# The bias line sent between two row halves, a seventh expert block in a free area, and a gather with its high parts first

## The chip, the core and the metric

The kernel runs on one core of a Trainium2 chip. The metric is the device time of one execution in microseconds. Five engines work side by side: TensorE (PE, with its weight loads PEld), VectorE (DVE), ScalarE (ACT), GpSimd (POOL) and SyncE (SP). They meet through semaphores. Transfers run on 16 DMA engines. SyncE's transfers form the queue q1, ScalarE's the queue q10.

## What is computed

The reference is a stack of two models on 256 tokens of width 1024, in fp32. Cut to what matters here:

```
# first block
z   = rms_norm(x) @ w_in                    # 1024 -> 1440: q_a, k_a, v_a, c_q, c_kv, k_rope
o_a = window attention(q_a, k_a, v_a)       # + rel_bias[t5_bucket(j - i)] on every score
o_b = latent attention(c_q, c_kv, k_rope)
x   = x + concat(norm(o_a), norm(o_b)) @ w_o
h2  = rms_norm(x)
aff = softmax(h2 @ w_router)                # 16 experts
gate, idx = top_k(aff.T, 32)                # every expert chooses 32 tokens
xe  = h2[idx]
ye  = (silu(xe @ w_gate) * (xe @ w_up)) @ w_down * gate
x   = x + scatter_add(ye)
# second block, two layers: mod = silu(c) @ ada_w + ada_b, four times; S5 mixer, conv FFN,
# forgetting attention, conv FFN, final norm
```

Each of the 16 experts has three weights of 1024 x 1024: 12 MB, six blocks of 2048 KB.

## The kernel before

Every engine has one hand-written program, and the order of work is the order of its lines. Weights come through `ring`, six slots of 16 KB per partition. `weight_plan` (L143) writes down the order of all loads and the slot of each. SyncE's program goes through this order in one loop: `begin` waits until what was last in the slot has been used (`released`, L210, says by which semaphore), and then the load is issued (L576). All loads are in this one queue, so a load that waits holds back all behind it.

Stages, in order:

- **First projection.** `x` is turned, and z is made in three column blocks (512, 512, 416), each in two row halves of 128 tokens (t = 0, 1). Block 0 is a plain fp32 product; blocks 1 and 2 work with high and low fp32r parts. ScalarE makes the high part of a weight block (`win_high`), VectorE the low one (`win_low`). The high part of block 2 goes to slot 0, so the load of block 2 waits for `z_mm` 2, both row halves of block 0.
- **The bias table.** One small product on TensorE (`line_mm`) makes a line of 511 values for each of 8 heads, and ScalarE copies it out, writes it to `bias_line` in DRAM and waits until it is there. Then it reads it back as `Lb`, 128 partitions x 8 heads x 384 values, each partition shifted by one (the spread, semaphore `line_spread`). The first `scores` wait for it.
- **Attention** in steps s = 0 to 7 of four heads (0 to 3 window attention, 4 to 7 latent attention). A step turns probabilities, spreads the inverse sums, makes the next step's scores, some filler product (`latent_product`, `wo_group`) and then its `outputs`.
- **ada.** 24 blocks of `ada_w` are multiplied with silu(c), six for each layer (`ada_product(n)`), then `ada_turn(layer)`. Products 0 to 11 are spread over the first block as fillers, each 16 matmuls on a ring block.
- **Routing.** The residual is turned and normed, logits, softmax, a search for the top 32 on VectorE, and from it the one-hot matrix `GallR`. The gather multiplies the rows, split in `xgh` and `xgl`, with `GallR`: eight chunks c of 128 features, each two row halves times two parts, into bank c % 7 of PSUM, and ScalarE copies each chunk out.
- **Experts.** For each expert six grouped products, j = 0 and 1 gate, 2 and 3 up, 4 and 5 down. Product j reads the ring slot of block j and frees it with `expert_mm`. In between are the sums, silu, and the scatter. GpSimd makes tables for the S5 stage beside them, one for every second expert. SyncE loads the next expert's block j when the current one's block j has been used.
- Then the S5 mixer, FFN, attention and FFN of the second block.

The order of the loads of interest in `weight_plan` before:

```
load("ada", 1, to=1); load("ada", 1, to=3)      # 4, 5
load("ada", 1, to=2); load("ada", 1, to=3); load("ada", 1, to=0)   # 6, 7, 8
load("ada", 1, to=1); load("ada", 1, to=2)      # 9, 10
load("expert", 2, NE, to=4)
load("ada", 1, to=3)                            # 11
load("expert", 4, NE, to=0)
```

Here are the functions that the change touches.

Of the kernel before, what the change touches and what calls it, by code (L numbers as in the profile page):

```python
# [20 lines left out]
F32 = mybir.dt.float32  # L21
# [8 lines left out]
P = 128  # L30
# [30 lines left out]
NE = 16  # L61
# [81 lines left out]
def weight_plan():  # L143
# [5 lines left out]
    def load(name, n=1, times=1, apart=False, to=None):  # L149
# [3 lines left out]
        first = sum(k[0] == name for k in order)  # L153
# [12 lines left out]
    def high_in(name, i, slot):  # L166

        high_slot[name, i] = slot
        before[name, i].append(holds[slot])
        holds[slot] = (name, i)  # L170
# [15 lines left out]
    load("ada", 1, to=3)  # L186
    load("ada", 1, to=0)
    load("ada", 1, to=1)
    load("ada", 1, to=2)
    load("expert", 2, NE, to=4)  # L190
    load("ada", 1, to=3)
    load("expert", 4, NE, to=0)
# [49 lines left out]
def build(nc, x, cons, cols, rows, relb, wrt, wff, bf16z, w_in, w_qb, w_kvb, w_o, w_gate, w_up, w_down, ada_w,  # L242
# [4 lines left out]
    with ExitStack() as ctx:  # L247
# [211 lines left out]
        xgh = SPLIT[:, 2 * D:2 * D + NT * D]  # L459
# [102 lines left out]
        def _(sp):  # L562
# [38 lines left out]
            for name, i in order:  # L601
# [4 lines left out]
                elif name == "ada":  # L606
                    load(begin(name, i), SLOT, block(ada_w, i))
                elif name == "qkvb":
# [3 lines left out]
                elif name == "expert":  # L612
                    begin(name, i)
                    expert(0, i)
                    if i == SLOTS - 1:
                        with sp.Fori(1, NE) as e:
                            for j in range(SLOTS):

                                sp.wait_ge(S("expert_mm"), e * SLOTS + (j + 1 - SLOTS))
                                expert(e, j)  # L620
                elif name == "s5":
# [19 lines left out]
        def _(pe):  # L641
# [123 lines left out]
            pe.wait_ge(S("line_loaded"), 32)  # L765
            mm(ps[0:AH, 6, 0:LINE], rb[:, :], K("onehot", BUCKETS + 1), True, True).then_inc(S("line_mm"), 1)
# [216 lines left out]
            for s in range(4, 8):  # L983
# [12 lines left out]
                if s == 5:  # L996
                    ada_turn(0)
                pe.wait_ge(S("r_copied"), s + 1)
                outputs(2 * s)
                outputs(2 * s + 1)  # L1000
            ada_product(6)
# [8 lines left out]
            ada_product(7)  # L1010
# [5 lines left out]
            ada_product(8)  # L1016
# [4 lines left out]
            for n in (9, 10, 11):  # L1021
                ada_product(n)
# [7 lines left out]

            pe.wait_ge(S("routed"), 4)
            pe.wait_ge(S("rows_low"), 1)
            for c in range(NC):
                if c == 7:

                    pe.wait_ge(S("xe_copied"), 1)
                for t in range(NT):
                    for part in (xgh, xgl):
                        last = mm(ps[:, c % 7, :], part[:, t * D + c * P:t * D + c * P + P], GallR[:, t, :],
                                  t == 0 and part is xgh, t == 1 and part is xgl)  # L1040
                last.then_inc(S("xe_mm"), 1)
# [4 lines left out]
            def expert(i, b):  # L1046
# [4 lines left out]
                def grouped(j, lhs, bank, first):  # L1051

                    w = filled("expert", j, i * 2 + b).rearrange("p (c n) -> p c n", c=4)
# [53 lines left out]
            with pe.Fori(0, NE // 2) as i:  # L1107
                for b in range(2):
                    expert(i, b)
# [177 lines left out]
        def _(act):  # L1287
# [135 lines left out]

# [67 lines left out]
            for s in range(4, 8):  # L1491
# [3 lines left out]
                if s > 4:  # L1495
                    spread_copied(s - 1)
# [1188 lines left out]
```

## Time and profile before

| | |
|---|---|
| median of three runs | 1448.74 us (1446.78 to 1451.35) |
| the profiled execution | 1453.92 us, its span 1452.1 us |
| TensorE busy | 1238.7 us, 85% |
| VectorE / ScalarE / GpSimd busy | 659.9 / 464.0 / 269.7 us |
| mean granted clock of TensorE | 0.888 of full speed |
| DMA | 369.62 MB, 255 GB/s in the mean |

A busy share is a mean over stages with different limits. The span is the profiled program on the core; the time of the execution has a little more around it. Times in the rows count from the start of the span.

### The profile page before, as it was taken

The numbers are of one execution on the slowest core, as the hardware profiler recorded it, in microseconds if no ns is written. First come the engines' busy times: TensorE is split into PE (matmuls) and PEld (weight loads), VectorE is DVE, ScalarE is ACT, GpSimd is POOL, SyncE is SP. The second block draws the span as 40 slices with busy tenths as digits, with TensorE's granted clock in tenths as the row PEclk, the third lists the DMA queues.
The fourth block names the chain that finished last, engine by engine and source line by source line (L and its number), as shares of the span: only waits on it lengthen the run. The fifth ranks groups of instructions, "written<-read, shape, count | busy, mean of one in ns | idle before, by whom it ended". The sixth has DMA issues, their size and how long they took to land.

```text
span 1452.1 us, 21871 instructions
## 1 busy us (share of the span) xinstructions
PE 1238.7 (85%) x8746; PEld 875.1 (60%) x8746; DVE 659.9 (45%) x1158; ACT 464.0 (32%) x682; POOL 269.7 (19%) x289
## 2 busy tenths in 40 slices
PE   7699988878788886887886779999969989899997
PEld 4455444333333332426655768999959767799995
DVE  2476452211211121214345636777763255676676
ACT  4364421111111111105313415444343243544442
POOL 0000376321303303113113600000016420000000
PEclk9899988987988898877976988999989959899998
DMA  6845699999999999993962214454344301355541
GB/s 247 370 174 232 246 397 429 428 428 429 427 429 429 428 429 429 428 429 148 395 247 107 88 58 160 178 200 182 147 174 153 138 30 35 132 196 194 196 173 44
DMA packets 36000, 369.62 MB, mean 255 GB/s; under 512 B 4069, under 2 KB 5614, under 8 KB 12270
## 3 DMA queue, kind: packets, MB, share of 16 engines
q1 hardware_dynamic: 33552, 364.66, 61.9%
q10 hardware_dynamic: 2398, 4.27, 0.8%
q8 instruction: 35, 0.57, 0.2%
q14 instruction: 15, 0.12, 0.0%
HBM read 367.84 MB, written 1.06 MB: 254 GB/s over the span
## 4 chain that ended last, share of the span: by engine, by line
PE 54%; DMA 28%; DVE 7%; ACT 4%; POOL 3%; issue 3%; DVEq 0%; SPq 0%; ACTq 0%; POOLq 0%
PE ps L649 52%; DMA ring<-in_w_up 24%; DMA W<-bias_line 2%; DMA ring<-in_w_in 1%; PE ps L664 1%; ACT ring_parts L488 1%; DVE W L2447 1%; PE ps L875 1%; DMA ring<-in_s_out 1%; DMA ring<-in_fox_in 1%; POOL ring_parts L496 0%; ACT XH L1352 0%; DVE ss L1913 0%; DVE W L2468 0%; DMA bias_line<-W 0%
## 5 line engine op out<-in xcount | busy, mean ns | idle before, releaser
L649 PE MATMUL ps<-W_parts 128*128 128x256 f32 (+1 forms) x2672 | 390.8, 309 | 8.7 <-issue 4.4
L649 PEld LDWEIGHTS ps<-W_parts 128*128 128x128 f32 x2672 | 363.2, 194 | 35.4 <-issue 10.3
L649 PE MATMUL ps<-ring,W 128*32 128x512 f32 (+2 forms) x1640 | 269.2, 721 | 77.5 <-DMA ring<-in_w_up 47.4
L649 PEld LDWEIGHTS ps<-ring,W 128*32 128x32 f32 (+1 forms) x1640 | 70.3, 131 | 249.9 <-issue 152.3
L649 PE MATMUL ps<-W 128*32 128x64 f32 (+7 forms) x1696 | 151.3, 324 | 51.6 <-DVE W L2455 22.5
L496 POOL TENSOR_TENSOR ring_parts<-ring,ring_parts 128x2048 fp32r<-128x2048 f32 x18 | 98.3, 5471 | 367.1 <-ACT ring_parts L488 330.3
L649 PEld LDWEIGHTS ps<-W 128*32 128x32 f32 (+5 forms) x1696 | 97.8, 178 | 110.4 <-issue 94.3
L2481 DVE TENSOR_TENSOR W_parts<-ring,W_parts 128x2048 fp32r<-128x2048 f32 x44 | 100.9, 2292 | 29.7 <-ACT W_parts L1645 29.7
L649 PE MATMUL ps<-XH_parts,ring_parts 128*128 128x256 f32 x512 | 96.6, 292 | 7.8 <-issue 5.0
L2362 DVE COPY W<-ps 128x1024 f32<-128x1024 f32 x16 | 19.6, 1224 | 173.7 <-PE ps L649 173.7
L649 PEld LDWEIGHTS ps<-kc,W 128*128 128x128 f32 x648 | 82.9, 209 | 10.4 <-issue 6.6
L649 PEld LDWEIGHTS ps<-XH_parts,ring_parts 128*128 128x128 f32 x512 | 83.4, 200 | 8.7 <-issue 5.6
L649 PE MATMUL ps<-kc,W 128*128 128x32 f32 (+2 forms) x648 | 84.1, 290 | 2.9 <-POOL W L1840 2.9
L1645 ACT ACTIVATE W_parts<-ring 128x2048 fp32r<-128x2048 f32 x44 | 83.6, 1900 | 0.0
L649 PE MATMUL ps<-ring_parts,W_parts 128*128 128x512 f32 (+1 forms) x256 | 72.3, 404 | 10.2 <-DVE W_parts L2470 10.2
L649 PE MATMUL ps<-W_parts,ring_parts 128*128 128x256 f32 x256 | 74.5, 291 | 0.0
L649 PEld LDWEIGHTS ps<-ring_parts,W_parts 128*128 128x128 f32 x256 | 49.7, 195 | 21.9 <-DVE W_parts L2470 10.4
L1847 POOL COPY W<-XH 128x256 f32<-128x256 f32 x14 | 5.6, 400 | 284.3 <-PE ps L649 284.3
L488 ACT ACTIVATE ring_parts<-ring 128x4096 fp32r<-128x4096 f32 x14 | 50.6, 3613 | 15.9 <-DMA ring<-in_fox_in 8.8
L2366 DVE COPY W<-ps 128x512 f32<-128x512 f32 x16 | 11.1, 692 | 95.4 <-PE ps L649 95.4
L2379 DVE TENSOR_TENSOR X<-X,ps 128x512 f32<-128x512 f32 x64 | 44.0, 687 | 22.9 <-PE ps L649 22.9
L2487 DVE TENSOR_TENSOR W_parts<-ring,W_parts 128x1024 fp32r<-128x1024 f32 x44 | 53.6, 1218 | 0.7 <-ACT W_parts L1653 0.7
(370 smaller groups left out, 1359.0 us busy)
## 6 DMA issues: line engine op xcount, KB each, us to landing
ring<-in_w_gate SPq DMA_DIRECT2D x32, 2048.0 KB, 22.2
ring<-in_w_up SPq DMA_DIRECT2D x32, 2048.0 KB, 26.5
ring<-in_w_down SPq DMA_DIRECT2D x32, 2048.0 KB, 23.4
ring<-in_ada_w SPq DMA_DIRECT2D x24, 2048.0 KB, 11.0
ring<-in_up SPq DMA_DIRECT2D x44, 1024.0 KB, 5.4
ring<-in_dn SPq DMA_DIRECT2D x44, 512.0 KB, 3.3
ring<-in_fox_in SPq DMA_DIRECT2D x6, 2048.0 KB, 8.2
ring<-in_w_in SPq DMA_DIRECT2D x2, 2048.0 KB, 13.7
```

The lines of the kernel that those rows point to most:

```text
L488: act.activation(ringr[:, high_slot[name], :], ring[:, slot_of[name], :], ACT.Copy).then_inc(S("w_high"), 1)
L496: eng.tensor_tensor(ringr[:, slot_of[name], a], ring[:, slot_of[name], a], ringr[:, high_slot[name], a].bitcast(F32), ALU.subtract).then_i ...
L649: return pe.matmul(o, l, r, start=a, stop=z_, skip_group_check=True, **kw)
L664: last = pe.transpose(ps[:, banks[c // 2], (c % 2) * T + t * P:(c % 2) * T + t * P + P], src[:, t, c * P:c * P + P], ident)
L875: last = pe.transpose(ps[:, 4 + g % 2, o:o + P], Pex[:, 2 * (g % 4) + h, kb * P:kb * P + P], ident)
L1645: act.activation(uh[:, b], ring[:, slot_of[name, b], 0:2048].rearrange("p (a n) -> p a n", a=2), ACT.Copy).then_inc(S("up_high"), 1)
L2362: v.tensor_copy(Us.rearrange("p (b n) -> p b n", b=2), ps[:, 2:4, :]).then_inc(S("u_copied"), 1)
L2366: v.tensor_copy(Ys[:, BANK:D], ps[:, 6, :]).then_inc(S("y1_copied"), 1)
L2379: tt(xs_part, xs_part, ps[:, k, :], ALU.add).then_inc(S("x_added"), 1)
L2447: last = tt(to[:, s], g, turn, ALU.mult)
L2481: tt(ul[:, b, :, :], ring[:, slot_of[f"up{k}", b], 0:2 * D].rearrange("p (a n) -> p a n", a=2), uh[:, b, :, :].bitcast(F32), ALU.subtract) ...
L2487: tt(dl[:, b, :], ring[:, slot_of[f"down{k}", b], 0:D], dh[:, b, :].bitcast(F32), ALU.subtract).then_inc(S("down_low"), 1)
```

## The change

1. `line_mm` is made after the row half t = 0 of projection block 0 instead of after t = 1. ScalarE copies the line out and sends it to DRAM before it copies the two halves of block 0 out. It asks for the spread behind these two copies (n == 0), not behind those of block 1, and makes `win_high(2, ...)` after that.
2. Block 0 of expert 0's `w_gate` is loaded into `O_`, the first 4096 columns of W, which is free from the last query turn (`qkb_turned` 4) until the S5 tables. Its request stands behind that of `ada` block 8. Slot 0 so begins with expert 1's block 0; the other five blocks of expert 0 and `ada` blocks 6 to 11 have other slots. The first two experts stand outside TensorE's loop. `ada_turn(0)` moves from step 5 to step 4, `ada_product(6)` and `(7)` into steps 6 and 7, in front of the outputs, and the later products move up by one.
3. The high parts of seven chunks are gathered first, then their low parts, then chunk 7. `xgh` lies in XH with the chunks apart. ScalarE makes it after the exponentials instead of before them, and VectorE makes `xgl` after `GallR` instead of before the search.

```diff
@@ weight_plan
     load("ada", 1, to=2)
-    load("ada", 1, to=3)
     load("ada", 1, to=0)
     load("ada", 1, to=1)
+    load("ada", 1, to=3)
     load("ada", 1, to=2)
-    load("expert", 2, NE, to=4)
-    load("ada", 1, to=3)
-    load("expert", 4, NE, to=0)
+    load("ada", 1, to=0)
+    for i, slot in ((1, 4), (2, 5), (3, 1), (4, 3), (5, 2)):
+        load("expert", 1, NE, to=slot, first=i)
+    load("expert", 1, NE - 1, to=0, first=0)
@@ SyncE
                     load(begin(name, i), SLOT, block(ada_w, i))
+                    if i == 8:
+
+                        sp.wait_ge(S("qkb_turned"), 4)
+                        sp.dma_start(O_, block(w_gate, 0)).then_inc(S("first_loaded"), 16)
...
-                    expert(0, i)
-                    if i == SLOTS - 1:
-                        with sp.Fori(1, NE) as e:
-                            for j in range(SLOTS):
-
+                    expert(0 if i else 1, i)
+                    if i == 0:
+
+                        with sp.Fori(1, NE - 1) as e:
+                            for j in range(1, SLOTS):
                                 sp.wait_ge(S("expert_mm"), e * SLOTS + (j + 1 - SLOTS))
                                 expert(e, j)
+                            sp.wait_ge(S("expert_mm"), e * SLOTS + 1)
+                            expert(e + 1, 0)
+                        for j in range(1, SLOTS):
+                            sp.wait_ge(S("expert_mm"), (NE - 2) * SLOTS + j + 1)
+                            expert(NE - 1, j)
@@ TensorE, first projection
-            pe.wait_ge(S("line_loaded"), 32)
-            mm(ps[0:AH, 6, 0:LINE], rb[:, :], K("onehot", BUCKETS + 1), True, True).then_inc(S("line_mm"), 1)
+                if t == 0:
+                    pe.wait_ge(S("line_loaded"), 32)
+                    mm(ps[0:AH, 6, 0:LINE], rb[:, :], K("onehot", BUCKETS + 1), True, True
+                       ).then_inc(S("line_mm"), 1)
@@ TensorE, steps 4 to 7
-                if s == 5:
+                if s == 4:
                     ada_turn(0)
+                elif s > 5:
+                    ada_product(s)
                 pe.wait_ge(S("r_copied"), s + 1)
                 outputs(2 * s)
                 outputs(2 * s + 1)
-            ada_product(6)
             wo_group(6)
@@ TensorE, gather
             pe.wait_ge(S("routed"), 4)
+            pe.wait_ge(S("rows_high"), 1)
+            for c in range(7):
+                gather(c, "high", True, False)
             pe.wait_ge(S("rows_low"), 1)
...
+            for c in range(7):
+                gather(c, "low", False, True).then_inc(S("xe_mm"), 1)
+            pe.wait_ge(S("xe_copied"), 1)
+            gather(7, "high", True, False)
+            gather(7, "low", False, True).then_inc(S("xe_mm"), 1)
@@ ScalarE, first projection
+            act.wait_ge(S("line_mm"), 1)
+            act.activation(lineS[:, 0:LINE], ps[0:AH, 6, 0:LINE], ACT.Copy).then_inc(S("line_copied"), 1)
+            act.wait_ge(S("line_copied"), 1)
+            act.dma_start(line_dram[:, 0:LINE], lineS[:, 0:LINE]).then_inc(S("line_written"), 16)
             act.wait_ge(S("rs_ready"), 1)
...
                 if n == 0:
-                    win_high(2, 0)
-                    win_high(2, 1)
-                if n == 0:
-                    act.wait_ge(S("line_mm"), 1)
-                    act.activation(lineS[:, 0:LINE], ps[0:AH, 6, 0:LINE], ACT.Copy).then_inc(S("line_copied"), 1)
-                    act.wait_ge(S("line_copied"), 1)
-                    act.dma_start(line_dram[:, 0:LINE], lineS[:, 0:LINE]).then_inc(S("line_written"), 16)
-                if n == 1:
                     act.wait_ge(S("line_written"), 16)
                     act.dma_start(Lb[:, :, :], bass.AP(line_dram.tensor, 0, [[1, P], [BANK, AH], [1, 384]])
                                   ).then_inc(S("line_spread"), 16)
+                    act.wait_ge(S("z_mm"), 2)
+                    win_high(2, 0)
+                    win_high(2, 1)
@@ ScalarE, routing
-            act.activation(xgh, XNf, ACT.Copy).then_inc(S("rows_high"), 1)
             act.wait_ge(S("routed"), 1)
...
+            for t in range(NT):
+                last = act.activation(xgh[:, :, t, :], XN[:, t, :].rearrange("p (c m) -> p c m", c=NC), ACT.Copy)
+            last.then_inc(S("rows_high"), 1)
             ada_copy(1)
@@ VectorE, routing
-            v.wait_ge(S("rows_high"), 1)
-            tt(xgl, XNf, xgh.bitcast(F32), ALU.subtract).then_inc(S("rows_low"), 1)
             v.wait_ge(S("route_mm"), 2)
...
             last.then_inc(S("routed"), 1)
+            v.wait_ge(S("rows_high"), 1)
+            for t in range(NT):
+                last = tt(xgl[:, t * D:t * D + D].rearrange("p (c m) -> p c m", c=NC),
+                          XN[:, t, :].rearrange("p (c m) -> p c m", c=NC), xgh[:, :, t, :].bitcast(F32), ALU.subtract)
+            last.then_inc(S("rows_low"), 1)
```

## Rows read from the trace of the kernel before

**Rows 1.** windows: start:end, us, busy time by engine, clock, DMA share, GB/s

```profile
...
18.50:30.00 11.50, 11.50 (x28) 4.65 (x27) 4.63 (x4) 6.24 (x6) 0.00 (x0) 1.00 0.08 15
30.00:51.00 21.00, 21.00 (x108) 17.89 (x110) 10.58 (x16) 7.54 (x9) 0.00 (x0) 1.00 0.97 401
...
54.00:68.00 14.00, 0.45 (x2) 0.48 (x4) 1.75 (x7) 2.35 (x4) 0.00 (x0) 0.64 1.02 431
...
142.00:159.00 17.00, 15.86 (x83) 7.41 (x81) 8.61 (x26) 5.98 (x17) 0.00 (x0) 1.00 0.00 0
...
250.00:600.00 350.00, 282.31 (x1871) 121.41 (x1863) 71.03 (x124) 49.50 (x68) 77.02 (x102) 0.85 1.01 428
```

**Rows 2.** chain that ended last, 600 to 700 us: start us, us, what

```profile
...
611.48 27.33 DMA ring<-in_w_up
```

**Rows 3.** timeline of PE, 0 to 80 us: start us, us, engine, operation, idle before

```profile
...
28.64 1.02 PE L649 MATMUL ps<-kc,rb 33*8 33x511 f32 x2
...
67.55 2.08 PE L649 MATMUL ps<-W 64*128 64x256 f32 x8 [14.33 <-DMA W<-bias_line]
69.56 2.30 PE L801 MATMUL ps<-kc,W 128*128 128x128 f32 x10
```

**Rows 4.** timeline of ACT, 0 to 100 us

```profile
...
44.08 0.41 ACTq L1421 DMA_DIRECT2D W<-bias_line  x1
...
54.40 0.47 ACT L1454 ACTIVATE W<-ps,pc 128x256 f32<-128x256 f32 x1
```

**Rows 5.** DMA issues, 28 to 70 us: size, us from issue to landing

```profile
...
W<-bias_line ACTq DMA_DIRECT2D x1, 1536.0 KB, 23.3
```

**Rows 6.** DMA queues, 51 to 54 and 54 to 58 us: packets, MB, share

```profile
...
q10 hardware_dynamic: 641, 0.98, 90.5%
q1 hardware_dynamic: 19, 0.26, 21.9%
...
q1 hardware_dynamic: 95, 1.56, 91.7%
q10 hardware_dynamic: 88, 0.12, 8.0%
```

**Rows 7.** timeline of SP's queue, 0 to 260 us

```profile
...
1.67 27.39 SPq L576 DMA_DIRECT2D ring<-in_w_in  x3
...
50.15 0.81 SPq L576 DMA_DIRECT2D ring<-in_ada_w  x2
...
203.22 2.05 SPq L576 DMA_DIRECT2D ring<-in_w_gate  x2
```

**Rows 8.** timelines of PE and DVE, 25 to 56 us

```profile
...
40.89 0.54 PE L649 MATMUL ps<-ring_parts,XH_parts 128*128 128x416 f32 x2
...
36.96 3.69 DVE L1969 TENSOR_TENSOR ring_parts<-ring,ring_parts 128x1664 fp32r<-128x1664 f32 x2 [12.19 <-ACT ring_parts L1384]
```

**Rows 9.** timeline of PE, 160 to 262 us

```profile
...
173.99 3.61 PE L649 MATMUL ps<-ring,silz 128*32 128x512 f32 x16
...
189.85 9.74 PE L649 MATMUL ps<-W_parts 128*128 128x512 f32 x32 [2.38 <-DVE W_parts L2306]
201.08 7.07 PE L649 MATMUL ps<-ring,W 128*32 128x512 f32 x64 [1.50 <-POOL W L1780]
```

**Rows 10.** timeline of PE, 140 to 162 us

```profile
...
145.89 1.09 PE L649 MATMUL ps<-W 128*64 128x128 f32 x16 [0.32 <-ACT W L1364]
...
156.25 1.92 PE L649 MATMUL ps<-ring,silz 128*32 128x512 f32 x16
159.04 3.24 PE L649 MATMUL ps<-ring,W 128*128 128x512 f32 x7 [0.87 <-ACT W L1376]
```

**Rows 11.** timelines of DVE and ACT in the routing and gather

```profile
...
178.66 2.28 DVE L2290 TENSOR_TENSOR W_parts<-XH,W_parts 128x2048 fp32r<-128x2048 f32 x1
...
174.30 1.91 ACT L1521 ACTIVATE W_parts<-XH 128x2048 fp32r<-128x2048 f32 x1
...
199.62 0.69 ACT L1533 ACTIVATE XH<-ps,pc 128x512 f32<-128x512 f32 x1 [0.22 <-PE ps L649]
```

**Rows 12.** timeline of PE in the second expert

```profile
...
246.10 3.68 PE L649 MATMUL ps<-kc,W 128*128 128x64 f32 x16 [2.90 <-POOL W L1840]
```

More of the change, by code:

```diff
@@ L147, in weight_plan, with load @@
     uses, holds, at = [0] * SLOTS, [None] * SLOTS, 0
-    def load(name, n=1, times=1, apart=False, to=None):
+    def load(name, n=1, times=1, apart=False, to=None, first=None):
         nonlocal at
         at = at if to is None else to
-        first = sum(k[0] == name for k in order)
+        first = sum(k[0] == name for k in order) if first is None else first
         for i in range(first, first + n):
@@ L168, in high_in @@
         high_slot[name, i] = slot
-        before[name, i].append(holds[slot])
         holds[slot] = (name, i)
@@ L455, in build @@
         xl = low_at(OT_AT)
-        xgh = SPLIT[:, 2 * D:2 * D + NT * D]
+        xgh = XHr[:, NT * D:2 * NT * D].rearrange("p (c t m) -> p c t m", c=NC, t=NT)
         xgl = SPLIT[:, 4 * D:4 * D + NT * D]
@@ L1009, in _ @@
             turn(0, X, (4, 5, 6, 2), "x_added")
-            ada_product(7)
+            ada_product(8)
             ht_ready(0)
@@ L1015, in _ @@
             last.then_inc(S("route_mm"), 1)
-            ada_product(8)
+            ada_product(9)
             pe.wait_ge(S("routed"), 2)
@@ L1020, in _ @@
             last.then_inc(S("route_mm"), 1)
-            for n in (9, 10, 11):
+            for n in (10, 11):
                 ada_product(n)
@@ L1028, in _, with gather @@
             last.then_inc(S("route_mm"), 1)
+            def gather(c, part, first, last_):
+                for t in range(NT):
+                    rows_ = xgh[:, c, t, :] if part == "high" else xgl[:, t * D + c * P:t * D + c * P + P]
+                    last = mm(ps[:, c % 7, :], rows_, GallR[:, t, :], first and t == 0, last_ and t == 1)
+                return last
             pe.wait_ge(S("routed"), 4)
+            pe.wait_ge(S("rows_high"), 1)
+            for c in range(7):
+                gather(c, "high", True, False)
             pe.wait_ge(S("rows_low"), 1)
[L1033 to L1041, printed above, removed]
+            for c in range(7):
[3 more added lines that the diff above has]
+            gather(7, "low", False, True).then_inc(S("xe_mm"), 1)
             pe.wait_ge(S("xe_copied"), 8)
@@ L1051, in grouped @@
                 def grouped(j, lhs, bank, first):
-                    w = filled("expert", j, i * 2 + b).rearrange("p (c n) -> p c n", c=4)
+                    if j:
+                        w = filled("expert", j, i * 2 + b)
+                    elif isinstance(i, int) and i * 2 + b == 0:
+                        pe.wait_ge(S("first_loaded"), 16)
+                        w = O_
+                    else:
+                        w = filled("expert", 0, i * 2 + (b - 1))
+                    w = w.rearrange("p (c n) -> p c n", c=4)
                     for n in range(2):
@@ L1105, in expert @@
                     pe.wait_ge(S("kc_copied"), i + 1)
-            with pe.Fori(0, NE // 2) as i:
+            for b in range(2):
+                expert(0, b)
+            with pe.Fori(1, NE // 2) as i:
                 for b in range(2):
@@ L1496, in _ @@
                     spread_copied(s - 1)
+                if s == 5:
+                    ada_keep(0)
                 if s == 6:
-                    ada_keep(0)
                     act.wait_ge(S("o_copied"), 6)
@@ L2309, in _ @@
             last.then_inc(S("routed"), 1)
+            v.wait_ge(S("rows_high"), 1)
+            for t in range(NT):
+                last = tt(xgl[:, t * D:t * D + D].rearrange("p (c m) -> p c m", c=NC),
+                          XN[:, t, :].rearrange("p (c m) -> p c m", c=NC), xgh[:, :, t, :].bitcast(F32), ALU.subtract)
+            last.then_inc(S("rows_low"), 1)
             def modulation(kept, a, b):
```

## The prediction

> **What bounds the kernel now.** I read the page's slices first, then `windows` over the stages, then the waits, and only then single instructions. The span falls into three kinds of stretch. In the sixteen experts the DMA engines are full: between 250 and 600 us they move 428 GB/s at a share of 1.01, while TensorE is busy for 282 of 350 us [rows 1]. The chain of work says the same: the last wait for a third projection block lasts 27.33 us and is a DMA [rows 2]. A 2048 KB block at 428 GB/s takes 4.9 us, so what is worth something there is a block that need not be moved in that stretch, or an earlier start of it. After the experts, and in the attention before them, TensorE sets the pace and everything behind it moves as one. The one large hole outside the experts is TensorE's wait for the bias table: 14.33 us, until 67.55 [rows 3].
>
> Why is that table late? ScalarE asks for the table, one row of 384 values per head spread to all partitions, at 44.08 [rows 4], and it takes 23.3 us to land [rows 5]. It is only 1536 KB, 3.7 us of a full DMA. It waits because it shares the engines. It consists of 128 x 8 pieces of 1,536 bytes, 64 for each of 16 engines; a block of SyncE's queue consists of 128 rows of 16 KB, 8 for each engine. Look at the packets by queue. From 51 to 54 us ScalarE's queue (q10) gets 641 packets and SyncE's (q1) only 19: there SyncE's queue was empty. From 54 to 58, with both filled, it is 88 against 95, one for one, and a pair costs an engine 4 x 16 / 95 = 0.67 us [rows 6]. So most of the table went through in a hole of 3 us, and the rest crept.
>
> **Part 1, the line sent between the row halves.** The line's product moves in front of the second row half. That half then ends 1.0 us later (the 1.02 us of the product at 28.64) [rows 3], and so do the two things that wait for it: SyncE's third projection load, whose issue ends at 29.06 now [rows 7], and ScalarE's copy of the second half. The write to DRAM goes out near 24, into an idle DMA (0.08 of its share from 18.5 to 30) [rows 1], and is back long before 30. But the table is asked for only behind ScalarE's copy of the second half: near 30.4, instead of 44.08. That is 0.7 us behind SyncE's load of 29.7, and two blocks of `ada` are in the same burst. From there SyncE's queue holds the third projection block, two `ada` blocks, `w_qb` and `w_kvb`, 8 packets each: 40 per engine.
>
> Now the sum of the queue. Before, this stream ran from about 30 to 51 and then left the hole until the next blocks, issued at 50.15 [rows 7], arrived at 54. After, it starts 1.0 us later and carries 35 to 39 packets of the table between its own, at 0.07 us each (3 us x 16 / 641) [rows 6]: 2.5 us. It ends at 54 to 54.5, and the next blocks are there: the hole is closed. 25 to 29 table packets per engine are left, and the queue holds 24 more of SyncE's (two `ada`, one `w_o`). At 0.67 us a pair that is 16 us and more: the table lands between 69 and 71.5, where all else that was issued lands. The lower end is an engine that still sees half a microsecond of hole, the upper one the slowest engine; the slowest decides, so I take 70.5. A second view of the same: the engines are full from 30 to 68 before and after [rows 1], carry the same bytes, and start 1.0 us later. So TensorE starts the scores 3.0 us **later** than at 67.55. The later landing of the third projection block (by 1.5 us) is hidden: VectorE ends its low half at 40.65, which becomes about 42.2, and TensorE, which begins this block at 40.89 with 0.54 us for each pair of products, reaches the half at about 43 [rows 8]. If this cover were short, the loss would be its excess.
>
> The Trainium skill (DMA: Bandwidth & Descriptors, Queues, rings and completion order) says that an engine takes turns between the queues, but drains a whole packet of some 9 to 17 descriptors before it switches. By it eight turns or fewer would serve the table, and the line would not be late at all (that is the first rival). The counts of the trace, 95 to 88, speak for one descriptor a turn.
>
> **Part 2, the seventh block.** `w_gate` block 0 goes to a free area as soon as the query turns are done, into DMA time that is partly idle (nothing moves from 142 to 159) [rows 1]. It leaves 87 blocks instead of 88 between the refill and the last awaited one: -4.9 us. But the first expert's first product now frees no slot; SyncE waits for the second. The refill began at 203.22, 2.1 us behind TensorE's start at 201.08 [rows 7, 9]; four products take 7.07 us [rows 9], so it is now 3.9 us behind: +1.8. The price is also TensorE's: `ada` products 6 and 7 stand in front of the outputs of steps 6 and 7. One costs 1.92 us; step 6 has 0.32 us of wait to hide it, step 7 none. Product 6 stood in front of the wait for `o_scaled`, which still ended last by 0.87 us [rows 10]: taking it out of there shortens nothing. I add 1.6 + 1.8 = +3.4. Bounds: 0 (hidden) to 3.8. `ada_turn` moved by one step lies in VectorE's waits: 0.
>
> **Part 3, the gather.** VectorE's subtraction (2.28 us) leaves the routing chain, and ScalarE's high copy (1.91 us) goes behind the exponentials [rows 11]. TensorE's `ada` product of 3.61 us ends at 177.6 [rows 9] and stands in front of the transposes, so it, not the sum of both, limits: VectorE's search starts near 178.1 instead of 180.94. -2.8 us. The low parts must then be made beside 14 high products; these take 14/32 of 9.74 us, 4.3 us [rows 9], the subtraction about 2.4: covered. But ScalarE's eight copies now start only behind the high parts: 8 x 0.69 = 5.5 us behind 4.5 make 10.0, where the gather took 9.74 and one copy (10.4) [rows 9, 11]. With hand-over times I take +0.5, between 0 and 1. So the experts start at 201.08 + 3.4 - 2.8 + 0.5 = 202.2.
>
> Refill: 202.2 + 3.9 = 206.1 against 203.22, +2.9; minus 4.9 gives **-2.0 us** for parts 2 and 3, between -5 (products hidden, copies not bunched) and 0. The cover is not wide: in expert 1 TensorE waits 2.90 us for GpSimd's table [rows 12], and the third expert's first slot comes free about 1 us before the DMA would run dry.
>
> **Sum.** +3.0 - 2.0 = +1.0 us on the profiled span of 1452.1. The profiled execution took 1453.92 against a median of 1448.74, so I put the sum on the median: **1449.7**, own range 1446.5 to 1452.5. The three runs shown are 4.6 us apart; 0.3% (4.3 us) is about what can be told from no change.
>
> **Rivals.**
> (a) *The table lands early* (0.25). If an engine serves several table packets a turn, or SyncE's second `ada` request waits behind the table's 1024 pieces so that a hole opens at 41, the table is there before 55. Then TensorE starts behind ScalarE's key copy, which ends at 54.87 [rows 4]: 12.7 us earlier. The granted clock, 0.64 in the mean of the wait [rows 1], need not fall to 1.2 GHz then: the first scores take 2.08 us and the turns behind them 2.30 [rows 3], at 2.4 GHz about half, so some 2 us more. -14.7 - 2.0: **1432**. For it: 3.7 us of bytes. Against it: the one-for-one counts.
> (b) *Half a hole* (0.13): a hole of 1 to 2 us stays at 54, even on the slowest engine; 15 to 29 packets slip through and the table lands at 58 to 66. -2 to -9 and -2: about **1441**.
> (c) *Slower* (0.10): the experts' refill is tied to TensorE, not to the count of blocks. If the path in front of the experts grows by more than 1 us beyond my sum, the slot for expert 3's first block comes free after the queue has run dry, and the -4.9 is given back; with the table at 71.5 this is +4 + 1.5: **1454**.
> (d) The forecast itself: 0.52.
>
> Faster by over 0.3% (below 1444.4): (a) and most of (b), 0.35. Within: (d) and the rest, 0.54. Slower: 0.11. For eight in ten the range must take in (a) and reach (c): 1431 to 1454.
>
> **What the profile after would show.** Right: the line's DMA near 24, the table's request near 30.4, but a landing time of about 40 us instead of 23.3, TensorE's wait 17 us, half clock until the scores. Between 51 and 54 q1 is not empty. SyncE's first refill 3.9 us behind the first expert product, a DMA gap of about 10 us before it. `ada` products inside steps 6 and 7 with no shorter wait for `o_scaled`. The routed search some 2.8 us nearer to the residual sum. Wrong: scores before 60, or a landing time under 25 us: then the sharing between the queues was misread, and this one term decides the sign of all.

## The result, and the profile after

The changed kernel takes 1436.4 us (median of six runs, 1428.91 to 1438.76), the kernel before 1450.49 us (six runs, 1446.78 to 1452.26). The ratio is 0.9897 [0.9875, 0.9919]: about 14 us or 1.0% **faster**, and the interval does not reach 1. I had forecast 1449.7 us and no difference that can be told. The profiled execution took 1438.76 us, its span is 1437.0 us, 15.1 us shorter than the 1452.1 us of before.

First the windows of the changed kernel, with the columns of [rows 1]:

```profile
18.50:30.00 11.50, 11.50 (x27) 4.42 (x26) 4.59 (x3) 6.21 (x6) 0.00 (x0) 1.00 1.00 412
30.00:42.00 12.00, 12.00 (x51) 9.35 (x50) 6.68 (x8) 4.34 (x4) 0.00 (x0) 1.00 0.58 211
...
142.00:159.00 17.00, 14.28 (x58) 6.21 (x57) 3.32 (x8) 3.74 (x9) 0.00 (x0) 0.90 0.48 165
```

The first line is the surprise. Between 18.5 and 30 us the DMA had a share of 0.08 before [rows 1]; now it is 1.00. Nothing that I had costed moves bytes there. SyncE's queue says what it is (start, us, operation):

```profile
1.67 1.85 SPq L576 DMA_DIRECT2D ring<-in_w_in  x3
3.56 1.01 SPq L576 DMA_DIRECT2D ring<-in_ada_w  x2
42.21 0.33 SPq L576 DMA_DIRECT2D ring<-in_w_qb  x1
```

The three projection loads were issued over 27.39 us [rows 7], because the third waited for the two row halves of block 0. Now all three are out at 3.52, and the two `ada` blocks behind them at 4.57. They are in before 33 us. In the third line `ada` and expert blocks move where nothing moved before, asked for near 147 and at 156.17; the seventh block itself is asked for already at 100.53, not in that gap. Next ScalarE's timeline, then the transfers from 33 to 41 us, and TensorE's timeline:

```profile
24.57 0.30 ACTq L1432 DMA_DIRECT2D bias_line<-W  x1
24.98 0.69 ACT L1441 ACTIVATE W<-ps,rs 128x512 f32<-128x512 f32 x1 [0.43 <-ACT W L1430]
31.02 0.69 ACT L1441 ACTIVATE W<-ps,rs 128x512 f32<-128x512 f32 x1 [5.36 <-PE ps L658]
33.30 0.41 ACTq L1445 DMA_DIRECT2D W<-bias_line  x1
33.81 3.08 ACT L1412 ACTIVATE ring_parts<-ring 128x1664 fp32r<-128x1664 f32 x2 [2.10 <-DMA bias_line<-W]
```

```profile
q10 hardware_dynamic: 1040, 1.57, 57.8%
...
W<-bias_line ACTq DMA_DIRECT2D x1, 1536.0 KB, 7.6
```

```profile
56.23 1.92 PE L658 MATMUL ps<-W 64*128 64x256 f32 x8 [1.90 <-ACT W L1481]
58.08 2.15 PE L812 MATMUL ps<-kc,W 128*128 128x128 f32 x10
```

The table is asked for at 33.30 and lands 7.6 us later, at 40.9. In those 8 us SyncE's queue, q1, has no packet at all; beside q10 there is only one packet of instructions. Before it took 23.3 us [rows 5]. So TensorE no longer waits 14.33 us for the bias table [rows 3] but 1.90 us for ScalarE's key copy, and starts the scores at 56.23 instead of 67.55: 11.3 us earlier.

Behind that the two kernels run nearly in step. TensorE, the refill, and the chain's last wait for a third projection block:

```profile
171.09 3.64 PE L658 MATMUL ps<-ring,silz 128*32 128x512 f32 x32
...
184.42 3.35 PE L658 MATMUL ps<-W_parts 128*128 128x512 f32 x14
...
190.71 1.92 PE L658 MATMUL ps<-W 128*32 128x512 f32 x16 [2.01 <-ACT XH L1563]
```

```profile
174.78 20.14 SPq L576 DMA_DIRECT2D ring<-in_w_gate  x2
196.25 1.91 SPq L576 DMA_DIRECT2D ring<-in_w_up  x2
```

```profile
599.52 25.76 DMA ring<-in_w_up
...
644.76 3.61 ACT ring_parts L488
```

The experts start at 190.71, 10.4 us earlier than in [rows 9], of which 11.3 came from the scores: 0.9 us were lost between. The first refill is the second of the two `w_gate` requests, issued about 194.6 (3.9 us behind the experts' start) against 203.22 [rows 7]: 8.6 us earlier. The last awaited block lands at 599.52 + 25.76 = 625.3 against 638.8 [rows 2]: 13.5 us, which is 8.6 and one block of 4.9. The last 1.6 us of the 15.1 come from behind it.

### The profile page after: what moved, and what is told of

Its sections match the earlier page's. It is cut to its first block, busy times and chain, and to the rows that moved or that the text cites. A ratio compares the mean times of both kernels' runs of the same rounds, so it can differ in the third digit from the quotient of the medians.

```text
span 1437.0 us, 21864 instructions
## 1 busy us (share of the span) xinstructions
PE 1232.7 (86%) x8746; PEld 876.6 (61%) x8746; DVE 668.7 (47%) x1159; ACT 463.6 (32%) x683; POOL 270.9 (19%) x289
## 4 chain that ended last, share of the span: by engine, by line
PE 58%; DMA 24%; DVE 7%; ACT 4%; POOL 3%; issue 3%; DVEq 0%; SPq 0%; ACTq 0%; POOLq 0%
PE ps L658 56%; DMA ring<-in_w_up 22%; ACT ring_parts L488 1%; PE ps L673 1%; DMA ring<-in_w_in 1%; DVE W L2480 1%; PE ps L886 1%; DMA ring<-in_fox_in 1%; DMA ring<-in_s_out 1%; POOL ring_parts L496 0%; DVE ss L1943 0%; DVE W L2501 0%; DVE XH L2078 0%; ACT XH L1380 0%; PE ps L898 0%
## 5 line engine op out<-in xcount | busy, mean ns | idle before, releaser
L658 PE MATMUL ps<-W_parts 128*128 128x256 f32 (+1 forms) x2656 | 385.4, 308 | 7.3 <-DVE W_parts L1970 3.1
L658 PEld LDWEIGHTS ps<-W_parts 128*128 128x128 f32 x2656 | 359.0, 193 | 32.2 <-issue 10.8
L658 PE MATMUL ps<-ring,W 128*32 128x512 f32 (+2 forms) x1624 | 265.7, 714 | 71.7 <-DMA ring<-in_w_up 39.3
L658 PE MATMUL ps<-W 32*128 32x64 f32 (+8 forms) x1712 | 149.2, 313 | 43.0 <-DVE W L2488 24.4
L658 PEld LDWEIGHTS ps<-W 32*128 32x128 f32 (+5 forms) x1712 | 94.4, 165 | 101.5 <-issue 85.1
L658 PEld LDWEIGHTS ps<-kc,W 128*128 128x128 f32 x648 | 88.4, 221 | 13.3 <-issue 13.3
L658 PE MATMUL ps<-kc,W 128*128 128x32 f32 (+2 forms) x648 | 89.3, 300 | 5.3 <-POOL W L1870 5.3
L1699 ACT ACTIVATE XH<-ps 128x256 f32<-128x256 f32 x44 | 16.9, 384 | 117.2 <-PE ps L658 117.2
```

Source lines behind the costliest of these rows:

```text
L658: return pe.matmul(o, l, r, start=a, stop=z_, skip_group_check=True, **kw)
L1699: act.activation(apd[:, b, 2:2 + T], ps[:, b, 0:T], ACT.Copy).then_inc(S("a_copied"), 1)
```

## What the diff shown ahead left out

The diff ahead of the prediction is an abridged one, and one line of the change is not in it. It is this, in `weight_plan`:

```diff
     def high_in(name, i, slot):
         high_slot[name, i] = slot
-        before[name, i].append(holds[slot])
         holds[slot] = (name, i)
```

`before[name, i]` lists what SyncE waits for ahead of a load. For the third projection block the removed line had put `z_mm` 2 there, because the *high part* of the block goes to slot 0, where block 0 lies. The load itself goes to slot 2, which is free. The changed kernel instead lets ScalarE wait for `z_mm` 2 ahead of `win_high(2, ...)`, which is the instruction that writes slot 0. I had listed that wait on ScalarE and had not asked which wait it replaced. My prediction kept "SyncE's third projection load, whose issue ends at 29.06 now" as a fixed part of the front.

## Experiments

Two theories. **L (the load):** the removed wait alone makes the table early, and my sum for the rest holds. **E (the early line):** it is early because the line is sent earlier, and I misread how two queues share an engine. Where the last microseconds matter I compare places in the trace rather than times; the reason follows below.

**1. The wait put back.** The changed kernel with the removed line restored; everything else as changed.

```diff
         high_slot[name, i] = slot
+        before[name, i].append(holds[slot])
         holds[slot] = (name, i)
```

> The changed kernel with one line put back: the third projection load waits again for both row halves of block 0, as the forecast had assumed. Theory L (the freed load decides; the sharing of the DMA engines was read rightly): the table is asked for near 31, shares with 40 packets of SyncE's per engine one for one and lands between 69 and 72, so the scores start at about 71 instead of 56.2, and the time is that of the kernel before within 4 us (parts 2 and 3 give 2, the table costs 3). Theory E (sending the line early is what gains, an engine serves several table packets a turn or a hole opens): the table lands before 50, the scores start near 56, and the time is that of the changed kernel, 13 us under before.

1449.5 us (10 runs), ratio to the kernel before 1.0006 [0.9985, 1.0026]. ScalarE, the transfers of 20 to 75 us, and TensorE in this run:

```profile
24.33 0.30 ACTq L1433 DMA_DIRECT2D bias_line<-W  x1
...
30.78 0.44 ACTq L1446 DMA_DIRECT2D W<-bias_line  x1
```

```profile
W<-bias_line ACTq DMA_DIRECT2D x1, 1536.0 KB, 39.2
```

```profile
70.08 2.08 PE L659 MATMUL ps<-W 64*128 64x256 f32 x8 [16.00 <-DMA W<-bias_line]
```

This is the kernel that my prediction described. It had, with the measured values in brackets, the line's write near 24 (24.33), the request near 30.4 (30.78), a landing time of about 40 us (39.2), a wait of 17 us (16.00), the table at 70.5 (70.0) and the total at 1449.7 (1449.5). The sending of the line alone makes the scores 2.5 us later than in [rows 3], not earlier. How far one execution can be trusted here: the first kernel of experiment 5 has the front of the kernel before and starts its scores at 65.88 instead of 67.55, and against it the cost is 4.2 us. Theory E falls. The two queues at one place of it, 41 to 51 and 51 to 54 us:

```profile
q1 hardware_dynamic: 311, 3.62, 86.0%
q10 hardware_dynamic: 312, 0.48, 12.8%
```

```profile
q1 hardware_dynamic: 140, 1.05, 83.8%
q10 hardware_dynamic: 139, 0.21, 19.4%
```

311 against 312 and 140 against 139: the queues get equal numbers of packets, a row of 8 to 16 KB against 1.5 KB. Equal numbers alone would also fit turns of several packets each. The bytes of 44 to 47 us, in 40 slices of 0.075 us, tell more:

```profile
GB/s 41 457 259 478 560 1550 0 478 0 41 457 259 478 560 1550 41 437 0 41 457 259 478 560 1550 20 457 0 41 437 239 300 778 1550 20 457 0 41 437 20 519
```

The pattern comes back every nine slices, 0.68 us, which is what a pair of one 16 KB row and one piece of the table was forecast to cost (0.67), and from 44.0 to 44.7 us there are 16 packets of each queue on the 16 engines. So a turn here is one packet. The Trainium skill (DMA: Bandwidth & Descriptors, Queues, rings and completion order) gives an engine's turn as a packet of some 9 to 17 descriptors; for these two queues the measurement says otherwise, and the bytes go 7.5 to 1 (3.62 against 0.48 MB) and 5 to 1 (1.05 against 0.21 MB) against the table. From 54 to 58 us this run has 106 packets of q1 and 231 of q10. That is the rest of the old hole, not another kind of turn: from 54 to 55 us it is 30 against 151, SyncE's queue running low, and from 55 to 58 us again 76 against 80.

**2. The load freed alone.** The kernel before with only that line removed: neither the line's new place, nor the seventh block, nor the gather.

```diff
-        before[name, i].append(holds[slot])
```

> The kernel before with only the third projection load freed; the line is sent and the table asked for where they were. Theory L: the two ada blocks move in the idle DMA before 33, so that the table, asked for near 42, meets only w_qb and w_kvb (16 packets per engine) and then an empty queue until 53: it lands near 53 and the scores start near 56, 11 us earlier; time 11 to 13 us under before. Theory E: without the early line the table lands at 60 or later; at most 6 us under before.

1433.88 us, ratio 0.9919 [0.9892, 0.9945]. This one line explains most of the result (0.9897). Its table is asked for late and lands late, and it doesn't matter:

```profile
40.91 0.44 ACTq L1420 DMA_DIRECT2D W<-bias_line  x1
```

```profile
W<-bias_line ACTq DMA_DIRECT2D x1, 1536.0 KB, 11.6
```

```profile
54.93 1.14 PE L648 MATMUL ps<-W 64*128 64x256 f32 x8 [1.91 <-ACT W L1453]
```

It is there at 52.5, before ScalarE's key copy ends.

**3. Part 1 whole.** Experiment 2 with the line made and sent between the row halves and spread at n == 0.

```diff
-            pe.wait_ge(S("line_loaded"), 32)
...
+                if t == 0:
+                    pe.wait_ge(S("line_loaded"), 32)
...
+                    act.wait_ge(S("z_mm"), 2)
+                    win_high(2, 0)
+                    win_high(2, 1)
```

> The kernel before with the whole of part 1 (line between the row halves, table asked for behind block 0, load freed) and nothing of parts 2 and 3. Scores near 56.2 as in the changed kernel: 11.3 us earlier, and up to 2 more if the clock does not fall; time 11 to 13 us under before. If parts 2 and 3 gave more than the 2 us forecast, this kernel stays more than 3 us over the changed one.

1437.18 us, ratio 0.9905 [0.987, 0.9941]. The table is asked for at 33.28, 7.6 us earlier than in experiment 2, takes 7.7 us, and the scores start at 54.80 instead of 54.93. With the load freed, the line's place is worth nothing; with the load held (experiment 1) it costs 2.5 to 4.2 us.

**4. Another cause for the same hole.** Experiment 1, with SyncE's wait kept and in addition the two `ada` requests and what follows held until the table is there.

```diff
+        before[name, i].append(holds[slot])
...
+                    if i == 0:
+                        sp.wait_ge(S("line_spread"), 16)
```

> As the first kernel of this set (load waits again), but SyncE asks for ada blocks 0 and 1 only when the table has landed. Theory L: the table then shares with 8 packets per engine of the projection block alone and lands near 39, so the scores wait for ScalarE's key copy again and start near 56: the time of the changed kernel within 3 us. Rival S (the table is slow by itself, its 1,536-byte pieces or the order of its rows, whatever is beside it): it takes over 20 us again.

1435.68 us, ratio 0.9914 [0.9888, 0.9941]. The table, asked for at 29.60, lands in 11.9 us beside the third projection load alone. Now the scores wait for something else:

```profile
57.16 2.08 PE L661 MATMUL ps<-W 64*128 64x256 f32 x8 [4.24 <-DMA ring<-in_w_qb]
```

Against experiment 1 they start 12.9 us earlier. So it is the SyncE bytes in the table's path that decide, not the instant of the request.

**5. Without part 1, and without part 2.** The changed kernel with the line, the spread and SyncE's wait as before (the first), and the kernel before with parts 1 and 3 but no block in the spare area (the second).

```diff
# first
+        before[name, i].append(holds[slot])
...
# second
-                    if i == 8:
...
-                        sp.dma_start(O_, block(w_gate, 0)).then_inc(S("first_loaded"), 16)
...
```

> The changed kernel without part 1: the bias line's write and spread, the wait of the third projection load on z_mm 2, and the place of the table's ask are as in the kernel before; the seventh block in the spare area and the gather's new order stay. The forecast's sum for parts 2 and 3 alone: the experts start about 1.1 us later, the first refill 2.9 us later, one block less of 4.9 us, so -2.0 us against the kernel before (between -5 and 0). If instead the gain of the changed kernel came from parts 2 and 3, it is over 5 us under the kernel before.

> The kernel before with part 1 (the freed third projection load included) and part 3 (gather order and the search's copies), without the seventh block. If part 2 nets to nearly nothing (one block of 4.9 us less against a refill 3.9 us instead of 2.1 us behind the experts' start and the ada products between the head turns), it equals the changed kernel within 2 us. If part 2 gains by itself, it is slower than the changed kernel by over 3 us.

Without part 1: 1447.27 us, ratio 0.9998 [0.9974, 1.0022]; I had -2.0 us, and -3.8 to +3.2 us are left by the interval. The parts 2 and 3 did not make the gain. Its trace shows no gain from them either: the last awaited block lands 571.8 us behind the start of the scores, against 571.3 us in the profiled run before. Without part 2: 1434.02 us, ratio 0.9886 [0.9852, 0.9919], level with the changed kernel. In this one TensorE met a wait for an `ada` block that the changed kernel's order of loads doesn't have, and VectorE, done with the search, then waited 3.02 us for TensorE, against 0.38 us in the changed kernel run again. These 2.6 us stand against the two products that part 2 puts in front of the outputs (3.4 us in the forecast), and the experts start 131.7 us behind the scores here and 132.1 there:

```profile
167.22 1.92 PE L648 MATMUL ps<-ring,silz 128*32 128x512 f32 x16 [1.92 <-DMA ring<-in_ada_w]
```

**6. The gather as it was.** The changed kernel, with ScalarE's high copy before the exponentials, the subtraction before the search, and high and low products in turn.

```diff
             v.wait_ge(S("rows_high"), 1)
             for t in range(NT):
                 last = tt(xgl[...], XN[...], xgh[...], ALU.subtract)     # ahead of the search again
```

> The changed kernel with the gather as it was: ScalarE's high copy ahead of the exponentials, VectorE's subtraction ahead of the search, high and low product in turn. The forecast's working says 2.8 us for the subtraction and the copy in the chain and 0.5 us given back for the bunched copies: about 2.3 us slower than the changed kernel. If the subtraction only moves to another place of the chain, no difference.

1434.33 us, 0.9886 [0.9856, 0.9915], beside the changed kernel on the same chip with 1433.81 us, 0.9883 [0.9854, 0.9912] (experiment 7). The experts start at 190.51, 135.7 us behind the scores, against 132.1 there: part 3 is worth 3.6 us at this place, where I had 2.3 (some of it may be the clock: between 165 and 175 us it was 0.56 here and 0.84 there). The search starts 3.5 us nearer to the residual's turns, where 2.8 was forecast, and from the search to the experts it is 20.2 us there and 20.3 here, so the bunched copies cost nothing where I had 0.5. At the last up block 2.3 us of it are left (569.5 against 567.2 us behind the scores), and the time shows nothing of it.

**7. The changed kernel again**, as a measure for 6 and 9.

> The changed kernel once more, beside the two below on one chip, as their measure: ratio to the kernel before 0.985 to 0.992.

Ratio 0.9883, beside the 0.9897 of the first comparison.

**8. Product 7 later.** In the changed kernel `ada_product(7)` stands in front of the outputs of step 7, and TensorE then waits 2.72 us for `o_scaled`. Here it stands in that wait.

```diff
+            ada_product(7)
             wo_group(6)
```

> The changed kernel with ada product 7 moved from between the output groups to just ahead of output-projection group 6, where TensorE waited 2.72 us for o_scaled; the product itself takes 1.92 us. If TensorE's work up to there sets the search and through it the experts' start, the time is 2 to 3.6 us under that of the changed kernel. If a transfer sets the experts' start, no difference.

> The changed kernel with ada product 7 ahead of output-projection group 6 once more, with more rounds. Its first run stood at 0.9843 of the kernel before, the changed kernel at 0.9897 and 0.9883. In the trace the experts start 129.3 us behind the scores instead of 132.1, so 2.8 us (0.2%) are explained by the moved product: 0.9843 to 0.987. If more than that was gained the first time, it was scatter of the stage behind the experts, and the ratio lies at 0.986 to 0.989.

The first time 1427.76 us, 0.9843 [0.9822, 0.9863]; again 1428.5 us, 0.9883 [0.9848, 0.9918]. The wait shrinks in both traces as expected; here the changed kernel (experiment 7) and this one (second time):

```profile
148.09 3.67 PE L658 MATMUL ps<-ring,W 128*128 128x512 f32 x8 [2.72 <-ACT W L1404]
...
155.48 2.10 PE L673 MATMUL ps<-kc,X 128*128 128x128 f32 x16
```

```profile
146.01 3.67 PE L658 MATMUL ps<-ring,W 128*128 128x512 f32 x8 [0.87 <-ACT W L1405]
...
153.40 2.10 PE L673 MATMUL ps<-kc,X 128*128 128x128 f32 x16
```

TensorE is 2.1 us further at the residual's turns, 1.8 us if both are counted from the start of the scores (55.20 and 54.95). But the experts start 129.3 us behind the scores in the first trace and 132.1 us in the second, exactly as in the changed kernel. The windows of 151 to 165, 165 to 175 and 175 to 188 us, of the first and of the second trace, say why:

```profile
151.00:165.00 14.00, 12.57 (x96) 7.38 (x98) 6.71 (x18) 11.28 (x21) 9.03 (x33) 1.00 1.00 405
165.00:175.00 10.00, 6.39 (x47) 3.41 (x40) 9.17 (x22) 1.23 (x3) 8.54 (x20) 0.89 1.01 427
175.00:188.00 13.00, 11.10 (x69) 6.97 (x71) 12.32 (x23) 6.25 (x10) 9.74 (x15) 0.95 0.73 309
```

```profile
151.00:165.00 14.00, 14.00 (x86) 7.70 (x85) 6.48 (x16) 10.68 (x20) 8.95 (x32) 0.83 1.01 403
165.00:175.00 10.00, 6.68 (x49) 2.63 (x46) 8.45 (x22) 1.97 (x4) 8.38 (x22) 0.84 1.00 424
175.00:188.00 13.00, 11.04 (x40) 8.00 (x43) 12.25 (x26) 6.01 (x9) 7.08 (x13) 0.76 0.76 320
```

The granted clock is 1.00, 0.89, 0.95 in the one and 0.83, 0.84, 0.76 in the other. The 16 matmuls of the `ada` product behind the logits take 1.92 us in the first trace and 3.64 us in the second. The 1.8 us won are in the program and can be lost to the clock of one execution.

**9. The spare area for expert 0's last block**, so that the first ring slot comes free with the first product, alone and with experiment 8's move.

```diff
-    for i, slot in ((1, 4), (2, 5), (3, 1), (4, 3), (5, 2)):
+    for i, slot in ((0, 4), (1, 5), (2, 1), (3, 3), (4, 2)):
...
-                        sp.dma_start(O_, block(w_gate, 0)).then_inc(S("first_loaded"), 16)
+                        sp.dma_start(O_, block(w_down, 1)).then_inc(S("first_loaded"), 16)
...
+            pool.wait_ge(S("expert_mm"), 6)
             table(0)
```

The area holds its block longer now, so GpSimd has to wait for the last product of expert 0 before its first table. That wait is new, and in these two versions it comes with the move.

> The changed kernel with the spare area holding expert 0's last block, and so the first freed slot read two blocks earlier: the first refill is issued about 2.1 us behind the experts' start instead of 3.9 us. If the chain of refills sets the end, 1.8 us under the changed kernel. If something else does, no difference.

> The changed kernel with ada product 7 just ahead of output-projection group 6 and with the spare area holding expert 0's last block. The two steps lie one behind the other on the same path (start of the experts, then the first freed slot), so if the chain of refills sets the end their gains add: 2 to 3.6 us and 1.8 us, 4 to 5 us under the changed kernel. If one covers the other, or if the refill then meets a slot that is not yet free or a late table of GpSimd, it is no more than 3.6 us.

Alone 1429.3 us, 0.9849 [0.9825, 0.9874]; both 1432.49 us, 0.9876 [0.985, 0.9902], level with the changed kernel's 0.9883 on that chip, where 4 to 5 us less were expected. In the run with both, the refill is where it should be, 2.0 us behind the first product:

```profile
184.55 7.07 PE L655 MATMUL ps<-ring,W 128*32 128x512 f32 x64 [2.09 <-ACT XH L1561]
```

```profile
186.53 2.04 SPq L576 DMA_DIRECT2D ring<-in_w_gate  x2
```

From the experts' start to the last landed up block it takes 434.6 us (593.46 + 25.66 - 184.55) against 435.1 (596.22 + 26.20 - 187.31) in the changed kernel: of 1.8 us expected 0.5 arrive. Most of the other 1.3 us went into a hole. In the run with both, the DMA engines ran dry from 242 to 244 us, about 1.7 us of them idle:

```profile
242.00:244.00 2.00, 2.00 (x26) 0.56 (x19) 0.00 (x0) 0.00 (x0) 0.00 (x0) 1.00 0.17 66
```

SyncE asks for expert 3's first block only at 243.09, because TensorE, in expert 1, had waited 4.96 us for GpSimd's table, and the slot comes free behind that. In the changed kernel run again the wait is 3.84 us and the share from 246 to 252 us is 0.88, some 0.7 us idle, so 1.0 of the 1.3 us are in the difference. With the block's move alone the wait is 2.50 us, there is no hole (a share of 1.02 from 242 to 244), and the stretch takes 433.6 us, 1.5 less than 435.1: there the 1.8 us nearly arrive. This is the thin cover that the prediction named, "about 1 us before the DMA would run dry". In sum the last block of the run with both lands 3.1 us earlier behind the scores, and the time shows 1.3 us of it, within its scatter. None of these versions is shown to beat the changed kernel.

**Why the times scatter so.** From ScalarE's first high copy of the S5 stage to the end of the span, all of these kernels do the same work. The stretch takes 795.7 us in the profiled run before, 792.2 in the changed kernel, 789.0 in it again, and 784.9 in experiment 1, the shortest of all. In the experiments it lies between 784.9 and 792.3. That is more than the effects of parts 2 and 3. Two lines of 760 to 811 us, before and in experiment 1:

```profile
760.00:811.00 51.00, 33.98 (x508) 29.26 (x509) 29.92 (x34) 21.60 (x19) 24.72 (x9) 0.70 0.24 95
```

```profile
760.00:811.00 51.00, 32.63 (x489) 29.36 (x482) 37.98 (x33) 20.19 (x18) 29.15 (x7) 0.80 0.15 57
```

The granted clock differs, 0.70 against 0.80. That the clock alone makes the whole spread is likely and not shown.

## Why the prediction was wrong

**The step that failed** is the first of part 1: that SyncE's third projection load keeps its wait, "whose issue ends at 29.06 now", and that "That half then ends 1.0 us later ..., and so do the two things that wait for it". In the changed kernel only ScalarE's copy waits; the load is out at 3.52. Everything that followed from a queue full from 30 us on was computed for another program. In place of +3.0 us the term is -11.3 us (67.55 to 56.23) in the pair of profiled runs, and -12.6 (to 54.93) in experiment 2, which is that edit alone.

**The working on top of it was right.** Experiment 1 is that program. Measured, with the forecast in brackets: the table at 70.0 (70.5), its landing time 39.2 (40), the scores 2.5 to 4.2 us later (3.0), the total 1449.5 (1449.7). One packet in turn for each queue is confirmed by the equal counts and the period of 0.68 us. The hole was closed but for one microsecond (54 to 55). The write "back long before 30" held there; in the changed kernel it met the freed loads in its engines, and small constants in its own queue that they had held up (726 packets of q10 were through by 24 us, 910 before), and took from 24.57 to about 33.2, 8.6 us for 16 KB, which moved the request by 2.3 us and cost nothing.

**Parts 2 and 3.** In the profiled pair: experts +0.9 us relative to the scores (forecast +1.1), refill +2.7 (forecast +2.9), one block less -4.9, together -2.2 (forecast -2.0). The agreement is luck in good part. The same sum is +0.6 us for the first kernel of experiment 5 against the kernel before (571.8 against 571.3 us from the scores to the last awaited block), and -1.6 us for the changed kernel run again against experiment 3 (567.2 against 568.8). Experiment 8 shows such a sum moving by 2.8 us with the clock of one run. Over the runs the stretch from the experts' start to the last up block is 437.7, 436.7, 437.0 and 438.6 us with the old order of loads (before, 2, 3, second of 5), and 433.8 to 436.7 in the eight runs with the new one (the changed kernel twice, 1, 4, first of 5, 6, both of 8), 435.3 in the mean: -2.2 us, where 1.8 - 4.9 = -3.1 was forecast. A part of the 0.9 us that are missing is DMA idle time in front of expert 3's first block (0.7 us in the changed kernel run again, 0.5 in the first of experiment 8); the rest stays open. Part 3 came out 1.3 us larger than its term (experiment 6): 0.7 in the search, 0.5 in the copies. The `ada` products ahead of the outputs of steps 6 and 7 were sized rightly, 1.5 and 1.8 us against 1.6 and 1.8; not in the sum was that TensorE, after its wait of 2.72 us, made eight matmuls of `wo_group` 6 in 5.37 us in the profiled changed kernel, and in 3.67 us in it again.

**The rivals.** Rival (a) had the time, 1432, and its ending: the table before 55, and then ScalarE's key copy, 11.3 us earlier instead of 12.7. Of its two causes neither is the real one, but the second, "a hole opens at 41", was close in kind: the hole is at 34 to 42. I gave it 0.25. The measured 1436.4 is outside the forecast's own range, 1446.5 to 1452.5, and inside the wide one, 1431 to 1454, only because that was drawn to take in this rival. The hole of rival (c), the experts' refill tied to TensorE, is there in small: 0.7 us in the changed kernel run again, 1.7 us in the last kernel of experiment 9. The mark that I named for this case, a landing time under 25 us, is what came (7.6); the cause that I tied to it, "then the sharing between the queues was misread", did not.

**The granted clock** in the stretch 18.5 to 51 is 1.00 before and after; between 54 and 68 before it was 0.64, with TensorE busy for 0.45 of 14 us [rows 1]. In the profiled changed kernel the first scores still took 1.92 us, at a granted clock of 0.56 and near the 2.08 of [rows 3]; in experiments 2 and 3 they took 1.14 and 1.13 us, in 2 at a granted clock of 1.00, which is 2.4 GHz. I had counted 2 us for this in rival (a); it comes in some executions and not in others.

## What to carry to other kernels

- Read a diff for the waits that vanish as well as for the instructions that move. A wait that appears on one engine can stand in for one taken off another. Ask which, because in a queue that is served in order the wait's removal moves every transfer behind it.
- Here a small transfer in a queue of its own got one turn for each turn of the bulk queue, 1.5 KB against 8 to 16. What made it early was not an earlier request but a moment in which the bulk queue was empty.
- When an edit is worth 1 to 3 us of 1440, compare distances between fixed points of the trace over several runs; the totals here could not tell it.

## What the runs showed of the hardware

VectorE and GpSimd slow each other down in a way that I had not costed. The changed gather moved VectorE's six table products into GpSimd's time. VectorE and then GpSimd in the changed kernel:

```profile
189.55 0.69 DVE L2377 TENSOR_TENSOR W<-W 128x512 f32<-128x512 f32 x1
190.28 0.77 DVE L2378 TENSOR_TENSOR W<-W 128x512 f32<-128x512 f32 x1
191.08 1.43 DVE L2379 TENSOR_TENSOR W<-W 128x512 f32<-128x512 f32 x1
192.54 1.43 DVE L2380 TENSOR_TENSOR W<-W 128x512 f32<-128x512 f32 x1
```

```profile
190.46 1.50 POOL L1794 TENSOR_TENSOR W<-W 128x512 f32<-128x512 f32 x1
192.04 1.39 POOL L1795 TENSOR_TENSOR W<-W 128x512 f32<-128x512 f32 x1
```

Both slow down. The same VectorE product takes 0.69 us alone and 1.43 us from the moment GpSimd works. GpSimd's first one takes 1.50 us here, and 1.05 in the kernel before, where the two do not meet:

```profile
200.81 1.05 POOL L1764 TENSOR_TENSOR W<-W 128x512 f32<-128x512 f32 x1
```

The Trainium skill (SBUF — State Buffer, SBUF: two separate sides) has the two engines take a shared pair of ports by turns when a VectorE operation has two inputs in SBUF, and the loser wait; the trace agrees that both wait. That each holds the ports for its whole length fits less well: a VectorE product and its neighbour on GpSimd take 1.46 us together (191.08 to 192.54), where 0.69 and 1.05 in strict turn would be 1.74.

It was off the path to the experts' start, which waited for ScalarE's last copy. It was not off the path behind it. TensorE gets GpSimd's table for expert 1 45.0 to 45.2 us behind the experts' start in the eight profiled runs in which the products do not meet, and 45.9 to 46.3 us in the four in which two or more of VectorE's do (the changed kernel twice, the first of 8, the last of 9); in the two in which one does it is 45.7. In those four it waits 3.84 to 5.36 us for that table, and on it hangs the slot of expert 3's first block.

The same operation and size in the same kernel can take 1.92 or 3.64 us, by the granted clock of that execution, in places that differ between executions (experiment 8).
